# C's decays added to its scores by a fourth matmul, input squares on ScalarE, and half the input remainders on VectorE, in a two-block float32 layer on one core

## What is computed

```python
h = rms_norm(x, norm_gain)                       # x * rsqrt(mean(x*x)) * gain
proj = einsum('bsd,de->bse', h, w_in)            # q, k, v and gates of A, B, C
# C, the forgetting attention, 8 heads of 64
logf = log_sigmoid(fc + b_forget)
c = cumsum(logf, axis=1)                         # per head, over the tokens
s = q @ k.T * d**-0.5
decay = c[query] - c[key]
s = where(dist >= 0, s + decay, -inf)
p = softmax(s, axis=-1)
yc = p @ v
# A: 4 heads, two maps each, bias -slope*dist; B: 8 heads, window of 128, a sink:
m = maximum(max(s), sink); e = exp(s - m); p = e / (sum(e) + exp(sink - m))
# then gates, three up projections, w_o, and the second block
```

## Time and profile before

| | us |
|---|---|
| median of three runs | 1279.6 |
| profiled execution, its own time | 1279.9 |
| its span, first to last instruction | 1278.1 |
| PE busy | 1234.3 (97%) |
| DVE busy | 658.9 (52%) |
| ACT busy | 550.4 (43%) |
| POOL busy | 659.0 (52%) |
| mean granted clock of PE | 0.987 |

### The profile page before, as it was taken

How to read it: one execution, slowest core, us unless ns; L and a number is a source line. 1 busy time by engine, 2 the same in 40 slices (tenths; PEclk the granted TensorE clock), 3 DMA queues, 4 the chain that set the end, 5 groups by cost and what they waited for, 6 DMA issues and landing times.

```text
span 1278.1 us, 17097 instructions
## 1 busy us (share of the span) xinstructions
PE 1234.3 (97%) x6230; PEld 982.5 (77%) x6230; DVE 658.9 (52%) x1217; ACT 550.4 (43%) x1066; POOL 659.0 (52%) x501
## 2 busy tenths in 40 slices
PE   7998989999999999999989999999999999999996
PEld 5886767777878888888776676878888888888885
DVE  6436744765743312125277545459999999200024
ACT  4544544676654333235552647542332333322344
POOL 4772223235346544446454464646767776655542
PEclk9998999999999999999988999999999999999998
DMA  5333222113222433343231121423333333433321
GB/s 197 112 113 98 67 61 73 50 50 83 67 66 83 114 92 91 95 152 112 82 84 50 42 71 53 116 82 84 99 99 99 90 92 87 128 96 94 100 74 66
DMA packets 63939, 113.94 MB, mean 89 GB/s; under 512 B 7016, under 2 KB 12776, under 8 KB 63856
## 3 DMA queue, kind: packets, MB, share of 16 engines
q1 hardware_dynamic: 63712, 112.84, 31.0%
q10 hardware_dynamic: 144, 0.00, 0.0%
HBM read 110.71 MB, written 2.11 MB: 88 GB/s over the span
## 4 chain that ended last, share of the span: by engine, by line
PE 83%; DVE 9%; ACT 3%; issue 2%; POOL 1%; DMA 1%; DVEq 0%; SPq 0%; ACTq 0%; POOLq 0%
PE pb L911 24%; PE pb L912 24%; PE pb L914 24%; PE pb L1065 2%; PE pb L1041 1%; DVE P L1774 1%; PE pb L1016 1%; POOL HL L2191 1%; DVE B L1644 1%; PE pb L979 1%; DVE U L1644 1%; DVE sq L1632 1%; PE pb L981 1%; PE pb L980 1%; POOL wlo L2191 1%
## 5 line engine op out<-in xcount | busy, mean ns | idle before, releaser
L2191 POOL TENSOR_TENSOR wlo<-raw,whi 128x512 fp32r<-128x512 f32 (+3 forms) x398 | 539.6, 1372 | 437.7 <-ACT whi L1247 437.5
L911 PE MATMUL pb<-HH,whi 128*128 128x512 f32 x968 | 391.4, 404 | 0.0
L912 PE MATMUL pb<-HL,whi 128*128 128x512 f32 x968 | 384.1, 397 | 0.0
L914 PE MATMUL pb<-HH,wlo 128*128 128x512 f32 x968 | 382.6, 395 | 0.0
L1247 ACT ACTIVATE whi<-raw 128x512 fp32r<-128x512 f32 (+3 forms) x398 | 233.2, 613 | 184.5 <-PE pb L914 156.5
L911 PEld LDWEIGHTS pb<-HH,whi 128*128 128x128 f32 x968 | 183.3, 189 | 47.0 <-issue 3.7
L914 PEld LDWEIGHTS pb<-HH,wlo 128*128 128x128 f32 x968 | 182.7, 189 | 42.6
L912 PEld LDWEIGHTS pb<-HL,whi 128*128 128x128 f32 x968 | 182.9, 189 | 42.2 <-issue 2.4
L1644 DVE SCALAR_TENSOR_TENSOR cv<-zf,vecs,cv 128x512 f32<-128x512 f32 x88 | 124.9, 1419 | 3.1
L1322 ACT ACTIVATE P<-P,stat 128x256 f32<-128x256 f32 (+3 forms) x96 | 51.1, 533 | 92.9 <-DVE stat L1639 68.9
L1635 DVE TENSOR_TENSOR X<-pb,X 128x512 f32<-128x512 f32 x24 | 16.6, 691 | 137.7 <-PE pb L914 137.3
(11 more groups left out here) (386 smaller groups left out, 1913.1 us busy)
## 6 DMA issues: line engine op xcount, KB each, us to landing
raw<-in_wall SPq DMA_DIRECT2D x362, 256.0 KB, 2.7
raw<-in_wall SPq DMA_DIRECT2D x16, 192.0 KB, 2.4
raw<-in_wall SPq DMA_DIRECT2D x8, 260.0 KB, 3.1
X<-in_xT SPq DMA_DIRECT2D x8, 256.0 KB, 5.3
N<-c_sums SPq DMA_DIRECT2D x8, 256.0 KB, 4.1
X<-in_xT SPq DMA_DIRECT2D x2, 1024.0 KB, 7.7
outT<-PP SPq DMA_DIRECT2D x8, 256.0 KB, 2.2
raw<-in_wall SPq DMA_DIRECT2D x12, 128.0 KB, 2.1
```

Source lines behind the costliest of these rows:

```text
L911: pe.do.matmul(b, hi, xh[k], start=start, stop=False)
L912: pe.do.matmul(b, hi, xl[k], start=False, stop=False)
L914: m = pe.do.matmul(b, lo, xh[k], start=False, stop=stop)
L2191: g.do.tensor_tensor(lo, x, hi.bitcast(F32), ALU.subtract).then_inc(*up(name, point))
```

## The change

- **Input squares.** `first(k)` on ACT now makes `Square` of x behind `mh[k]`; DVE keeps `ml[k]` and the sum. DVE's sum waits for ACT's square, ACT's square for DVE's sum of two steps before.
- **`lambda`** moves from behind `first` to behind `columns1`, after tile qC0.
- **Remainders.** `hl[k]` of the odd k moves from POOL to DVE, inside DVE's own `x_norm` steps.
- **Decays.** c and -c are each split in hi (ACT) and lo (DVE). SP copies the rows, head by head, to two buffers of 128x2048: `AQ` holds in rows 0 to 3 (even heads) and 64 to 67 (odd heads) c hi, c lo, 1, 1; `AK` holds 1, 1, -c hi, -c lo. These are 32 DMAs of one row of 512 floats each, in a new step `decay` inside tile qC3. POOL sets both buffers to 1 at the start. Each C group gets a fourth pair of matmuls, of four rows, from `AQ` and `AK`. `cq`, `Nr`, `scratch`, `c_minus` and B's building for C go; the mask comes from `DC`, 384 columns of zeros in front of `maskC` in `CST`, whose load grows from 1280 to 1664 columns.
- **Maxima.** The reduction scales by -1 and takes the minimum, so it yields the negative maximum at once; the exponential reads its input with scale -1. A and C lose the operation on 128x1; B's changes to a minimum with `no_sink`.

```diff
@@ stages
-        add("lambda")
...
         add("columns1")
+        add("lambda")
...
-        self.tile("main", ("qC", 3))
+        self.tile("main", ("qC", 3), between=lambda i: add("decay") if i == 4 else None)
         add("out", "qC", 3)
-        take("S", ("cq",))
-        add("cq")
@@ tensor, pair
+                if kind == "C":
+                    pe.wait_ge(*at("decay_in"))
+                    for s in range(2):
+                        rows = slice(64 * s, 64 * s + 4)
+                        pe.do.matmul(ps(*tiles[s])[:, 0:wd], AQ[rows, T * t + P * i:T * t + P * i + P],
+                                     AK[rows, T * t:T * t + wd], start=False, stop=True).then_inc(
+                            *up("scored", ("full", tiles[s])))
@@ scalar
+                if k > 2:
+                    a.wait_ge(*at("sq_step", k - 2))
+                a.do.activation(sqs[(k - 1) % 2] if k else acc, xk[k], ACT.Square).then_inc(*up("a_norm", ("sq", k)))
...
+            def decay():
+                a.wait_ge(*at("c"))
+                a.do.activation(cum_hi, cT[0:8, :], ACT.Copy).then_inc(*up("a_small", ("cum_hi",)))
+                a.do.activation(neg_hi, cT[0:8, :], ACT.Copy, scale=-1.0).then_inc(*up("a_small", ("neg_hi",)))
@@ vector, x_norm
+                for n in {2: (1,), 4: (3,), 6: (5,), 7: (7,)}.get(k, ()):
+                    v.wait_ge(*at("x_hi", n))
+                    v.do.tensor_tensor(hl[n], sqs[n % 2], hh[n].bitcast(F32), ALU.subtract).then_inc(
+                        *up("v_lo", ("x_lo", n)))
@@ vector, scores
-                    fused(bb[:, P * i:P * i + P], Nr[h % 4][:, P * i:P * i + P], cq, maskC, ALU.add, ALU.add,
-                          *[("neg_used", h)] * (i == 3), name="v_soft")
-                    if i:
-                        affine(bb[:, 0:P * i], Nr[h % 4][:, 0:P * i], cq, None, ALU.add, None,
-                               *[("neg_used", h)] * (i == 3), name="v_soft")
+                    bias = DC[:, 384 - P * i:512]
...
-                    v.do.tensor_tensor_reduce(Pr[s % 6][:, 0:wd], ps("scores", *u, m)[:, 0:wd], bias, 1.0, LOWEST,
-                                              ALU.add, ALU.max, stat(u, 4 * m)).then_inc(
+                    v.do.tensor_tensor_reduce(Pr[s % 6][:, 0:wd], ps("scores", *u, m)[:, 0:wd], bias, -1.0, -LOWEST,
+                                              ALU.add, ALU.min, stat(u, 0 if kind == "B" else 4 * m + 1)).then_inc(
@@ pool
+            def begin():
+                for x in (AQ, AK):
+                    g.do.memset(x[0:68, :].bitcast(F32), 1.0).then_inc(*up("g_set", ("decay_ones",)))
@@ sync
+            def decay():
+                s.wait_ge(*at("decay_ones"))
+                for dst, row, hi, lo, name in ((AQ, 0, cum_hi, cum_lo, "cum"), (AK, 2, neg_hi, neg_lo, "neg")):
+                    for i, (part, x) in enumerate((("hi", hi), ("lo", lo))):
+                        s.wait_ge(*at(f"{name}_{part}"))
+                        for half in range(2):
+                            r = 64 * half + row + i
+                            for t in range(4):
+                                s.do.dma_start(dst[r:r + 1, T * t:T * t + T].bitcast(F32),
+                                               x[2 * t + half:2 * t + half + 1, :].bitcast(F32)).then_inc(*landing("landed_decay", ("decay_in",)))
```

More of the change, by code:

```diff
@@ L718, in build @@
         wlo = [ar(f"wlo{i}", BLK * P + 8, F32R) for i in range(NS)]
-        CST = ar("cst", 128 * 4 + 512 + 256)
+        CST = ar("cst", 128 * 3 + 2 * 512 + 256)
         CU8 = ar("cu8", MASKS, U8, 1)
@@ L778, in build @@
                     head_l[n, t] = like(f"{n}l{t}", lo, dt=F32R)[:, :]
+        cum_hi, cum_lo, neg_hi, neg_lo = (like(f"cum{n}", n, dt=F32R)[0:8, :] for n in ("W1", "th1", "W2", "th2"))
+        AQ, AK = (tensor_at(f"decay_{n}", [P, 4 * T], F32R, place[n + "0"]) for n in ("vA", "qB"))
         yhi, ylo = {}, {}
@@ L798, in build @@
         base_q, base_k = gs, F3
-        RGW = like("RGW", "cst", 6 * P, skip=512 * 4)
+        RGW = like("RGW", "cst", 6 * P, skip=896 * 4)
         acc1, acc2, r2 = (third(U3, i) for i in range(3))
@@ L991, in forget_rows @@
                 i.then_inc(*up("small", ("full", ("sums",))))
-            def forget_columns():
-                free(("cq",))
-                pe.wait_ge(*at("c"))
-                for m in range(4):
-                    i = pe.do.matmul(ps("cq")[:, 8 * m:8 * m + 8], cT[0:8, P * m:P * m + P], ident[0:8, 0:8],
-                                     start=True, stop=True)
-                i.then_inc(*up("small", ("full", ("cq",))))
             def pair(one, two):
@@ L2270, in half_out @@
                         *up("g_res", ("final", d, half)))
-            follow({"split": split, "out": out_tile, "x_norm": x_norm, "gate_out": gate_out, "masks_in": masks_in, "begin2": begin2,
+            follow({"begin": begin, "split": split, "out": out_tile, "x_norm": x_norm, "gate_out": gate_out, "masks_in": masks_in, "begin2": begin2,
                     "norms2": norms2, "level": level, "cv_out": cv_out, "residual": residual,
@@ L2340, in end @@
                     s.wait_ge(*at("stored", i))
-            follow({"split": lambda u: load(u + NR), "begin": begin, "sums": sums, "pre": pre, "masks": masks,
+            follow({"split": lambda u: load(u + NR), "begin": begin, "decay": decay, "masks": masks,
                     "x_again": x_again, "begin2": begin2, "p_in": p_in, "half_out": half_out, "end": end})
```

95 lines of the change are left out of this document (38 added, 57 removed).

## The result

The changed kernel took **1289.0 us** (median of four runs, 1287.1 to 1290.4), the kernel before 1279.2 (four runs). The ratio is 1.0078, 95% interval 1.0062 to 1.0094: about 10 us **slower**, where the prediction said 4 us faster. The profiled execution spans 1286.2 us, 8.1 more than before, at a mean granted clock of 0.985 (before 0.987).

The account below looks back on a forecast made before the run. TensorE (PE) was taken to bound the kernel, with its waits up to 300 us. Terms -5.2 - 1.1 + 9.1 + 2.5 - 7.2 + 2.5 + 1.1 - 5.5 = -3.8 us from 1279.9 gave 1276.1, stated as 1276.0; range 1266 to 1281.

Parts of the forecast that it names:

- point 3: C's start: 32 row copies at 0.445 us each on SyncE make TensorE wait, +9.1 us, plus +2.5 for low clock.
- point 5: C's 16 groups: fourth matmul pairs cost +2.5 us, and their changes of row shape +1.1 us.
- point 7: Off the path: odd remainders on VectorE, memsets, splits of c and lambda behind columns1 were costed at nothing.
- Point 1: First stage: TensorE no longer waits for ScalarE's whi near 24 us; -5.2 us, bounds -4.5 and -5.9.
- Point 2: Before C's start: TensorE's transposes of cT go away, -1.1 us.
- R2: Rival on the row copies: dear, slower overall from 0.65 us per copy on; at 0.8 us, 1287; chance 0.10.
- R1: Rival on the row copies: cheap, issued in under 0.15 us each, so no wait, 1264.4; chance 0.12.
- The clock's loss: After the wait at C's start: work at half clock loses +2.5 us, between 1.7 and 3.4.
- Point 4: C's second step and the tile behind it: former waits for VectorE and half clock disappear, -7.2 us.
- Point 6: Later softmax steps, 112 to 300 us: VectorE's relief shortens TensorE's waits, -5.5 us, bounds -3 and -9.

Follow-up runs that it names:

- 64 rows: The changed kernel with the fourth matmul contracting 64 rows (60 of them zero on the keys' side) instead of four: ratio 1.0058 to the kernel before, 1286.6 us.
- late lambda: The changed kernel with the lambda step moved from behind columns1 to behind qC2's evacuation: ratio 1.0052 to the kernel before, 1286.1 us.
- the first stage's moves alone: The kernel before with input squares on ScalarE and lambda behind qC2's evacuation, C's decays unchanged: ratio 0.9959, 5.2 us faster.

## Why the prediction was wrong, point by point

The profiled execution was forecast at 1276.1 us and took 1288.0, 11.9 more. Three steps failed: the price of a row copy (point 3, a mis-sized term, 5.3 us of wait), the fourth pairs with their change of row shape (point 5, mis-sized, 3.5 us), and the new place of `lambda`, put at nothing (point 7, a wrong mechanism, 2.3 us). Another 1.4 us arose behind 300 us. The other differences come to -0.6.

**Point 1, first stage: right.** -5.9 against -5.2, within the bounds; no wait for `whi`, norm1 at 29.72 (forecast 30.1 + 0.3). What the prediction didn't say is that the move of lambda would have given only 1.9 without the squares' move: the text costed the squares on ScalarE as a burden, and they are what makes VectorE's `ML` timely.

**Point 2: right,** -1.1.

**Point 3, the row copies: the main error, a mis-sized term.** Place and mechanism were right, and the size was not. The working was 32 x 0.445 + 2.0 against PE's start. Measured: 0.63 us for each, 1.7 from issue to landing. The forecast's own sum is 0.2 too high: with 31 steps from the first issue to the last, 89.6 + 31 x 0.445 + 2.0 is 105.4 and the wait 8.9. The measured price adds 31 x (0.63 - 0.445) = 5.7 and the landing takes 0.3 off, 14.3 against the 14.4 of the trace: the rest of the working (SyncE free behind unit 33, PE at the third pair, all moved by the same shift) held. The bounds, 0.327 to 0.475, came from loads of 128 rows; a copy of one row was never bounded from above, though the prediction itself named it as something that the trace has not. Of R2, *copies are dear*, with its threshold of 0.65 us per copy (0.64 by the working's own numbers, since 1282.2 - 1276.0 is 6.2), the observed value is just short; the time came out slower all the same, through this term together with points 5 and 7. R1 is refuted: even the least of the 32 is 0.575 us. The 50 ns that the prediction took from the Trainium skill, DMA: Bandwidth & Descriptors, Anatomy of one DMA, are the sequencer's dispatch of a DMA that GpSimd issues; SyncE and ScalarE issued the copies here, so no run here tests the figure, and it was no price for them. The clock's loss was forecast as 2.5 and is 2.4.

**Point 4: right in kind and nearly in size,** -6.0 with the second step's fourth pairs in it, -6.7 without, forecast -7.2. No wait took its place.

**Point 5: mis-sized.** The pairs' own work was right (64 rows: 0.2 us in the first step and 2.1 in the seven others, 2.3 in all, forecast 2.5). The change of shape was put at 24 x 0.09 / 2 = 1.1, with 2.2 as the upper end. It is 3.6 in seven steps: 0.10 us at the entry and 0.10 to 0.20 at the exit of each of 14 pairs. The halving was a guess between bounds, and the upper end, 0.09 from the row of a change that the kernel before had, was no upper end either. The wide steps were to grow by 0.4 to 0.6 and grew by 1.0. The rule on tiling modes in the Trainium skill (TensorEngine Tiling (Array Packing), Key Properties) pointed to the upper end, and the measurement lies beyond it.

**Point 6: right in kind, and in size by luck.** The steps of C without a fourth pair are 4.0 us shorter than before (from the third step on), A's part is -1.5: 5.5 as forecast, which was half of 11 between bounds of 3 and 9. It was hidden under the fourth pairs: of the three narrow steps two became 0.8 us shorter and one 0.15, where all were forecast at about 1. The sign operation's share is 1.7 us in the time, mostly in A and in C's narrow steps.

**Point 7: the step that failed in its mechanism.** "`lambda` behind `columns1`: DVE and ACT have slack of several us there." VectorE has slack there by its busy time; POOL has none: from 42.5 to 72 us its longest idle time in the changed kernel is 0.18 us. I asked which engine waits at that place and not which queue is full behind it, and took the dot products at their old price. 2.0 us, by the experiment; 2.3 in the ledger. What I had left to the range for the remainders on VectorE was the wrong suspect, before the run and once more after it.

The sum by measured terms: -5.9 + 2.3 - 1.1 + 14.4 + 2.4 + 0.9 + 0.5 (first step's pairs and the slower matmuls round the wait) - 6.0 + 5.0 - 4.0 - 1.5 = 7.0, against 6.7 in the ledger at 300 us. Another 1.4 us arise behind it, in code that the change leaves alone: 0.7 between 657 and 700, 0.2 at 1099 and 0.5 behind the last matmul. The 0.7 are +2.1 and -1.4. The +2.1 begin with POOL's first `wlo` of a tile, here before and after, with TensorE's wait for it:

```profile
656.01 1.12 POOL L2191 TENSOR_TENSOR wlo<-raw,whi 128x384 fp32r<-128x384 f32 x1 [12.97 <-ACT whi L1247]
657.28 0.66 PE L979 MATMUL pb<-whi,HH 128*128 128x384 f32 x1 [4.62 <-POOL wlo L2191]
```

```profile
662.68 2.36 POOL L2190 TENSOR_TENSOR wlo<-raw,whi 128x384 fp32r<-128x384 f32 x1 [12.99 <-ACT whi L1247]
665.19 0.66 PE L979 MATMUL pb<-whi,HH 128*128 128x384 f32 x1 [5.88 <-POOL wlo L2190]
```

Where POOL's operation takes 1.12 us, VectorE's scaling of `gs` beside it takes 1.15; where POOL's takes 2.36, that scaling takes 0.34 and VectorE's next three operations run through first. One engine or the other goes first. Of the 14 traces ten have the short form, three the long one (the changed kernel, late lambda, and the first stage's moves alone), and the one with 64 rows lies between, with 1.69. Kernels with C as before and with C changed stand on both sides, so I take it for chance in the timing and not for an effect of the change; no run shows what decides it. The -1.4 come near 700, where the mean granted clock over 8 us is 0.79 and before 0.57. The median is 9.7 above, of which the profiled pair shows 8.1.

## What to carry to other kernels

Price a DMA by the issue, on the engine that issues it: many small copies in a row cost that engine and whoever waits for the last one, however few bytes they hold. Before moving bytes between partitions, ask whether the matmul can select them: rows kept where they are, zeros around them, a selector on the other side.

When a step is moved "into slack", look at what each engine has queued behind the new place, and above all at the fullest queue that is fed through it. Slack of the engine that executes the step isn't the slack of the chain.

If a matmul with a few rows stands between matmuls of 64, give it 64 rows with zeros: here a pair of 64 rows took no longer than the score pair ahead of it (0.11 us at 128 columns, 0.17 at 384), and the change of shape took 3.6 us in 14 pairs.

## What the runs showed of the hardware

- A copy of one row of 2 KB from SBUF to SBUF occupies its issuing engine 0.59 us, 0.63 from start to start; a load into 128 partitions 0.33 alone (a weight unit) and 0.445 in a row of four (`Nr`). Fewer bytes, longer issue. SyncE and ScalarE issue side by side at 0.63 us each, as SyncE does alone.
- A pair of matmuls of four rows between pairs of 64 costs 0.26 us at 128 columns and 0.37 at 384, and 0.10 us more in front; with 64 rows of the same columns, 0.11 and 0.17.
- VectorE's dot product of 128x64 takes 0.22 us in the kernel before and 1.34 beside a POOL subtraction of 1.29; a VectorE subtraction on SBUF 0.68 and 1.8; POOL's 1.30 and 1.74. Both sides lose.
- A column repeated by a step of zero as stationary operand costs no more than a full one: 0.11 us a pair at 128 columns (91.67 to 91.78).
